# Reordering the opening of a hybrid encoder kernel: x first, small loads on three queues, gate products turned round

## The reference

```
hn = rms_norm(h, norm_mix[0])            # h = x
proj = hn @ w_in                         # 2048 x 12352: q, k, v, z, and 32 + 32 gate columns b, a
qkv = silu(causal_depthwise_conv(qkv, conv_w))       # 4 taps
q = l2_normalize(q); k = l2_normalize(k)
beta = sigmoid(b)
g = -exp(a_log) * softplus(a + dt_bias)
o = gated_delta_rule_chunked(q, k, v, g, beta)       # uses cumulative sums of g
```

## Time and profile before

| | us |
|---|---|
| median of 3 runs | 3359.17 (3358.46 to 3363.18) |
| profiled execution, its time | 3362.38 |
| its span in the trace | 3360.7 |
| PE busy | 3197.1 (95% of the span) |
| DVE busy | 2268.7 (68%) |
| ACT busy | 1694.3 (50%) |
| POOL busy | 807.8 (24%) |

### The profile page before, as it was taken

The page is one execution under the profiler, slowest core; times in us unless marked ns, Lnnn a source line. Parts: engine busy times, 40 slices in busy tenths (PEclk is TensorE's granted clock), DMA queues, the critical chain, the costliest instruction groups (busy, mean ns, idle before and its releaser), DMA issues.

```text
span 3360.7 us, 62145 instructions
## 1 busy us (share of the span) xinstructions
PE 3197.1 (95%) x19134; PEld 2793.7 (83%) x19134; DVE 2268.7 (68%) x4217; ACT 1694.3 (50%) x3583; POOL 807.8 (24%) x1362
## 2 busy tenths in 40 slices
PE   5999999999989999999999988988999999999987
PEld 5898989898878888888888876877888888888875
DVE  4677777777755688667877756865667655775555
ACT  3556565666654555444545545324555444554443
POOL 0000000000010288788888810761000000000000
PEclk7999999999999999999999999988999999999998
DMA  4444444444347777777777856996666676666743
GB/s 124 117 114 130 113 122 115 123 111 131 106 135 192 193 198 207 196 219 194 204 208 192 213 153 166 269 236 174 178 186 184 180 187 177 186 187 179 187 123 112
DMA packets 1061823, 564.78 MB, mean 168 GB/s; under 512 B 59536, under 2 KB 1049744, under 8 KB 1061232
## 3 DMA queue, kind: packets, MB, share of 16 engines
q1 hardware_dynamic: 995808, 500.79, 55.6%
q10 hardware_dynamic: 57568, 37.50, 3.8%
q0 software_dynamic: 8368, 25.51, 2.5%
HBM read 532.49 MB, written 31.23 MB: 168 GB/s over the span
## 4 chain that ended last, share of the span: by engine, by line
PE 76%; DVE 9%; DMA 7%; issue 4%; ACT 3%; SPq 2%; ACTq 0%; DVEq 0%; POOL 0%; POOLq 0%
PE bank L288 42%; PE bank L289 21%; PE bank L665 5%; DVE w_lo L276 4%; DMA raw<-in_ple_w_gate_dram 3%; DMA z_scratch<-z 2%; ACT w_hi L270 1%; DVE normed L1923 1%; DVE tiles L1911 1%; PE bank L663 1%; DVE tiles L303 1%; SPq L491 1%; SPq L505 1%; ACT mid L968 1%; PE bank L726 0%
## 5 line engine op out<-in xcount | busy, mean ns | idle before, releaser
L288 PE MATMUL bank<-act,w_hi 128*128 128x512 f32 x4352 | 1594.6, 408 | 54.0 <-DVE w_lo L276 41.6
L276 DVE TENSOR_TENSOR w_lo<-raw,w_hi 128x512 fp32r<-128x512 f32 x1856 | 1298.6, 748 | 244.0 <-ACT w_hi L270 232.1
L289 PE MATMUL bank<-act,w_lo 128*128 128x256 f32 x4352 | 1223.4, 281 | 0.0
L288 PE MATMUL bank<-mid,w_hi 128*128 128x512 f32 x3072 | 1096.9, 401 | 27.7 <-DVE mid L1925 13.5
L270 ACT ACTIVATE w_hi<-raw 128x512 fp32r<-128x512 f32 x1856 | 1038.9, 619 | 145.4 <-PE bank L289 65.5
L288 PEld LDWEIGHTS bank<-act,w_hi 128*128 128x128 f32 x4352 | 825.1, 190 | 258.8 <-DVE w_lo L276 57.1
L289 PE MATMUL bank<-mid,w_lo 128*128 128x256 f32 x3072 | 866.3, 282 | 0.0
L289 PEld LDWEIGHTS bank<-act,w_lo 128*128 128x128 f32 x4352 | 828.8, 190 | 4.0 <-issue 3.8
L288 PEld LDWEIGHTS bank<-mid,w_hi 128*128 128x128 f32 x3072 | 583.4, 190 | 171.9 <-DVE mid L1925 14.7
L289 PEld LDWEIGHTS bank<-mid,w_lo 128*128 128x128 f32 x3072 | 586.7, 191 | 0.0
L298 ACT ACTIVATE tiles<-bank 128x256 f32<-128x256 f32 x384 | 145.4, 379 | 574.7 <-PE bank L289 572.0
(11 more groups left out here) (311 smaller groups left out, 2995.6 us busy)
## 6 DMA issues: line engine op xcount, KB each, us to landing
raw<-in_mlp_w_up_dram SPq DMA_DIRECT2D x128, 1024.0 KB, 6.4
raw<-in_mlp_w_down_dram SPq DMA_DIRECT2D x128, 1024.0 KB, 6.0
raw<-in_gdn_w_in_dram SPq DMA_DIRECT2D x96, 1024.0 KB, 5.8
raw<-in_gdn_w_out_dram SPq DMA_DIRECT2D x32, 1024.0 KB, 6.2
raw<-in_ple_w_gate_dram SPq DMA_DIRECT2D x32, 1024.0 KB, 6.0
raw<-in_s_w_out_dram SPq DMA_DIRECT2D x28, 1024.0 KB, 6.8
raw<-in_s_w_in_dram ACTq DMA_DIRECT2D x10, 1024.0 KB, 11.8
c_scratch<-c_pow ACTq DMA_DIRECT2D x32, 256.0 KB, 4.4
```

Of the source, the lines that this page charges most:

```text
L276: eng.tensor_tensor(w_lo[par][:, c], raw[slot][:, c], w_hi[par][:, c].bitcast(F32), ALU.subtract).then_inc(S("lo_ready"), 1)
L288: eng.matmul(a[:, :], w_hi[par][:, w], rhs[:, k0 + kt, :], start=(k0 + kt == 0), stop=False)
L289: mm = eng.matmul(a[:, 0:NT], w_lo[par][:, w], rhs[:, k0 + kt, 0:NT], start=False, stop=(k0 + kt == kend - 1))
```

## The change

It rewrites the opening only; from the first round of the main loop on the instructions are the same.

- **Loads.** SP loads x in two halves with the constants between them, then chunks 0 and 1. ACT's queue takes nine small loads: three for S5 (`lam_in`, together with the constants) and six vectors (`params_in`). POOL's queue takes ten: the convolution taps, the gate weights, biases and masks (`side_in`).
- **x.** Scaled x goes to a buffer of its own (`xs`) and is turned first; raw x is turned after chunk 1, with h0 copied by ACT then.
- **Gates.** High and low gate weights lie side by side as one 128-column stationary operand, the 512 columns of `act` stream past: 16 matmuls. ACT copies the result out, and four small matmuls against a doubled identity (`cf[:, 15, :]`) turn it back and add the parts, after the first quarter of chunk 0.
- **S5 parameters.** DVE does a first part before x is scaled, a second beside chunk 0 and the gate values, and the rest after splitting chunk 2.
- **Order.** The sums of g come after chunk 1 and raw x, their transpose after the second quarter of chunk 2. Chunks 1 and 2 are split ahead of the loop over chunks; in it chunk n+3 is split after the convolution of chunk n (on DVE) and ahead of the tanh (on ACT). `gcT` is copied by ACT before it splits chunk 3.

Cut to its core:

```diff
...
+LAM_PARAMS, N_PARAMS, SIDE_PARAMS = 4, 6, 10
...
+        sb("four_pairs", [P, 4, 2 * NT], F32, g4b)
+        ba_out = sb("ba_out", [P, 2 * NT], F32, g4b)
+        xs = sb("xs", [P, 2, D], F32, g4b)
+        h0 = sb("h0", [P, KT, NT], F32, g4b)
...
+        ba_hl = mid[:, 0:4, :].rearrange("p a n -> p (a n)").rearrange("p (k s n) -> p k s n", k=KT, s=2)
...
+            x_rows = t["x"][0].rearrange("(b p) d -> b p d", p=P)
+            sp.dma_start(xn[:, 0, :], x_rows[0]).then_inc(S("x_in"), 16)
+            sp.dma_start(consts[:, :], t["constants"][:, 0:256]).then_inc(S("lam_in"), 16)
+            sp.dma_start(xn[:, 1, :], x_rows[1]).then_inc(S("x_in1"), 16)
             for n, col in enumerate((0, 2048, 4096, 4096 + P)):
                 if n == 2:
                     sp.wait_ge(S("ba_lo"), 1)
...
-            pe.wait_ge(S("params_in"), 16 * N_PARAMS)
-            for i in range(4):
...
+            def turn_x(src, again):
+
...
+                    if g >= 4:
+                        pe.wait_ge(*((S("h0_ready"), g - 3) if again else (S("act_ready0"), 2 * (g - 4) + 2)))
...
+                                              src[:, b, (2 * g + a) * P:(2 * g + a + 1) * P], ident)
                     mm.then_inc(S("x_turned"), 1)
+
+            pe.wait_ge(S("lam_in"), 16 * LAM_PARAMS)
+            pe.transpose(F[:, 0:P], rows[:, 3, :], ident)
+            pe.wait_ge(S("steps_ready"), 1)
+            pe.transpose(F[:, P:P + 64], rows[0:64, 4, :], ident[0:64, 0:64]).then_inc(S("vectors_turned"), 1)
+            pe.wait_ge(S("params_in"), 16 * N_PARAMS)
+            pe.transpose(A[:, 0:P], rows[:, 0, :], ident).then_inc(S("vectors_turned"), 1)
+            pe.wait_ge(S("x_scaled"), 2)
+            turn_x(xs, False)
+            pe.wait_ge(S("side_in"), 16 * SIDE_PARAMS)
+            for i in (1, 2):
+                mm = pe.transpose(A[:, i * P:(i + 1) * P], rows[:, i, :], ident)
+            mm.then_inc(S("vectors_turned"), 1)
 
             pe.wait_ge(S("act_ready0"), KT)
...
-            pe.wait_ge(S("vectors_ready"), 2)
...
-                for kt in range(KT):
-                    x_hi, x_lo = act[:, kt, b * P:(b + 1) * P], act[:, kt, NT + b * P:NT + (b + 1) * P]
-                    pe.matmul(A[:, b * 64:(b + 1) * 64], x_hi, bh[:, kt, :], start=(kt == 0), stop=False)
-                    pe.matmul(A[:, b * 64:(b + 1) * 64], x_lo, bh[:, kt, :], start=False, stop=False)
-                    mm = pe.matmul(A[:, b * 64:(b + 1) * 64], x_hi, bl[:, kt, :], start=False, stop=(kt == KT - 1))
+            pe.wait_ge(S("vectors_ready"), 3)
+            for kt in range(KT):
+                mm = pe.matmul(A[:, :], ba_hl[:, kt, :, :].rearrange("p s n -> p (s n)"), act[:, kt, :], start=(kt == 0),
+                               stop=(kt == KT - 1))
             mm.then_inc(S("ba_done"), 1)
...
+            def ba_turn():
+
+                pe.wait_ge(S("ba_out"), 2)
+                for b in range(2):
+                    for half_ in range(2):
+                        mm = pe.matmul(A[:, b * 64:(b + 1) * 64], ba_out[:, half_ * NT + b * P:half_ * NT + (b + 1) * P],
+                                       cf[:, 15, :], start=(half_ == 0), stop=(half_ == 1))
+                mm.then_inc(S("ba_done"), 1)
...
                     multiply(pe, n, q, n % 2, n % 2, act, tile_free=(n - 1) if (n >= 2 and q == 0) else None)
-                if n == 0:
-
-                    pe.wait_ge(S("setup_vectors"), 7)
+                    if n == 0 and q == 0:
+                        ba_turn()
+                    if n == 2 and q == 1:
+                        pe.wait_ge(S("setup_vectors"), 8)
+                        pe.transpose(F[0:64, 0:P], ga[:, 0, :], ident).then_inc(S("gc_turned"), 1)
+                if n == 1:
+                    turn_x(xn, True)
+                    pe.wait_ge(S("setup_vectors"), 6)
+                    pe.wait_ge(S("h0_ready"), 8)
                     g_all = ga[:, 8, :]
                     pe.matmul(B[:, 0:64], U, g_all, start=True, stop=True)
                     pe.matmul(B[:, 64:128], ones, g_all, start=True, stop=True).then_inc(S("gc_done"), 1)
-                if n == 1:
-                    pe.wait_ge(S("setup_vectors"), 8)
-                    pe.transpose(F[0:64, 0:P], ga[:, 0, :], ident).then_inc(S("gc_turned"), 1)
                 if n == 2:
...
+            params = [(rows[0:64, 3, :], t["s5_lam_re"][0].rearrange("(q g) p -> q (g p)", g=2), "lam_in"),
+                      (rows[64:128, 3, :], t["s5_lam_im"][0].rearrange("(q g) p -> q (g p)", g=2), "lam_in"),
+                      (ls2[0:64, 0:2], t["s5_log_step"][0].rearrange("(q g) -> q g", g=2), "lam_in"),
...
+            for dst, src, name in params:
+                se.dma_start(dst, src, allow_slow_non_contiguous=dst.shape[-1] == 1).then_inc(S(name), 16)
+            se.wait_ge(S("vectors_turned"), 1)
+            link(A_(cf[:, 0:2, :].rearrange("p a b -> p (a b)"), F[:, 0:P]))
+            A_(cf[:, 2, :], F[:, P:P + 64], ACT.Exp).then_inc(S("vectors_ready"), 1)
             for b in range(2):
+                se.wait_ge(S(("x_in", "x_in1")[b]), 16)
...
-            A_(bh, ba_w[:, :]).then_inc(S("ba_hi"), 1)
+            A_(vec[:, :], A[:, 0:P]).then_inc(S("vectors_ready"), 1)
+            for q in range(QUARTERS):
+                split_hi(se, 0, q, 0, 1, reused=False, par=0)
...
+                se.wait_ge(S("x_turned"), kt // 2 + 1)
...
+            se.wait_ge(S("side_in"), 16 * SIDE_PARAMS)
+            A_(ba_hl[:, :, 0, :], ba_w.rearrange("p (k n) -> p k n", k=KT)).then_inc(S("ba_out"), 1)
+            for q in range(QUARTERS):
+                split_hi(se, 1, q, 1, 1, reused=False, par=1)
+            se.wait_ge(S("vectors_turned"), 3)
+            A_(conv_w[:, :, :].rearrange("p a b -> p (a b)"), A[:, P:3 * P]).then_inc(S("vectors_ready"), 1)
+            se.wait_ge(S("ba_done"), 1)
+            A_(ba_out[:, :], A[:, :]).then_inc(S("ba_out"), 1)
...
-            se.wait_ge(S("ba_done"), 1)
+            A_(abias[:, 2, :], abias[:, 0, :], ACT.Exp).then_inc(S("setup_functions"), 1)
+            se.wait_ge(S("ba_done"), 2)
             v = A[:, 0:P].rearrange("p (b k h) -> p b k h", b=2, k=2)
             gv = lambda i: ga[:, i, :].rearrange("p (b h) -> p b h", b=2)
             A_(gv(0), v[:, :, 0, :], ACT.Exp, scale=-1.0).then_inc(S("setup_functions"), 1)
-            A_(abias[:, 2, :], abias[:, 0, :], ACT.Exp).then_inc(S("setup_functions"), 1)
+            se.wait_ge(S("setup_vectors"), 4)
+            A_(ga[:, 5, :], ga[:, 4, :], ACT.Exp, scale=-1.0).then_inc(S("setup_functions"), 1)
             se.wait_ge(S("setup_vectors"), 5)
...
             A_(ga[:, 6, :], ga[:, 5, :], ACT.Ln).then_inc(S("setup_functions"), 1)
+            for q in range(QUARTERS):
+                split_hi(se, 2, q, 2, 1, par=0)
+            se.wait_ge(S("setup_vectors"), 3)
+            A_(cf[:, 11, :], cf[:, 10, :], ACT.Sin)
+            A_(cf[:, 12, :], cf[:, 10, :], ACT.Sin, scale=0.5).then_inc(S("setup_functions"), 1)
+            A_(cf[:, 13, :], cf[:, 13, :], ACT.Sin).then_inc(S("setup_functions"), 1)
+            for g in range(8):
+                se.wait_ge(S("x_turned"), 8 + g + 1)
+                se.wait_ge(S("x_squared"), 2)
+                A_(h0[:, 2 * g:2 * g + 2, :].rearrange("p k n -> p (k n)"), (C, Dk, E, F)[g % 4][:, :]).then_inc(S("h0_ready"), 1)
...
-            for n in range(4):
-                for q in range(QUARTERS):
-                    split_hi(se, n + 1, q, (n + 1) % 3, (n + 1) // 3 + 1, reused=n + 1 >= 2, par=(n + 1) % 2)
...
+            for n in range(3):
+                half_copy(se, n + 1, n, n % 2, first=n < 2)
+                if n == 0:
+                    se.wait_ge(S("gc_turned"), 1)
+                    A_(gcT[0:64, :], F[0:64, 0:P]).then_inc(S("gc_turned_out"), 1)
                 if n < 2:
+                    for q in range(QUARTERS):
+                        split_hi(se, n + 3, q, (n + 3) % 3, 2, par=(n + 3) % 2)
                     gate_tanh(n, n % 2, y[:, n, :], "conv_done", n + 1, n < 2)
                 if n == 1:
                     squares(0, 2)
-                    se.wait_ge(S("gc_turned"), 1)
-                    A_(gcT[0:64, :], F[0:64, 0:P]).then_inc(S("gc_turned_out"), 1)
                 if n == 2:
+                    inverse_lengths(0, False)
                     decays(0)
...
+            side += [(ba_w.rearrange("p (k n) -> p k n", k=KT), w_in_d[:, :, 12288:12352]),
...
+            for dst, src in side:
+                gp.dma_start(dst, src, allow_slow_non_contiguous=dst.shape[-1] == 1).then_inc(S("side_in"), 16)
...
+            ve.wait_ge(S("lam_in"), 16 * LAM_PARAMS)
...
-            ve.wait_ge(S("x_squared"), 3)
-            link(ve.reciprocal(stat[:, 4:6], stat[:, 2:4]))
-            ve.wait_ge(S("x_turned"), 8)
-            for b in range(2):
-                TS(xn[:, b, :], xn[:, b, :], stat[:, 4 + b:5 + b], None, ALU.mult).then_inc(S("x_scaled"), 1)
...
-            ve.wait_ge(S("vectors_ready"), 2)
```

(57 more changed lines are left out.)

121 lines of the change are left out of this document (24 added, 97 removed).

## The result

The changed kernel takes 3341.33 us (median of 6 runs, 3328.85 to 3348.04) beside 3358.82 for the kernel before (6 runs, 3346.95 to 3365.65). The ratio is 0.9947, 95% interval 0.9922 to 0.9973: 17.8 us faster, 9 to 26 (the ratio applied to 3358.82). The forecast was 3336 in a range of 3331 to 3343.

What follows compares the result with a forecast made beforehand. The bound was when the main loop's first transpose starts, PE being busy from 108.5 us on. Earlier gate start 17.5 plus shorter gates 14.2 less 8.1 behind them gave 23.6 us: 3336, range 3331 to 3343.

Steps and rivals of the forecast that it cites:

- First term: Opening, before the root: the three S5 loads on ACT's queue land at 7.5 us, bounds 6.1 to 8.4.
- Rival (a): First stretch: S5 loads, parameters or chunk 0 held up by x, plus Exp's table; 3 to 5 us later, 3339 to 3341; 0.15.
- the queues: Small loads off SP's queue: exactly issue time is saved, the 11.6 us between 0.9 and 12.50.
- Second term: From the gates' end to the main loop's first transpose: 48.8 us instead of 40.7, 8.1 lost.
- The new order: Behind the gates: the rearranged work makes that stretch 48.8 us instead of 40.7, a loss of 8.1.
- Both waits: PE idles some 7 us between chunk 1 and chunk 2, and 7 us before the squared lengths, queued ahead of chunk 3.
- The tables: ACT's table loads take 1.28 us each, with no added drain of 1.38 us.
- the 3343 of that rule: Five table loads on the new chain with a 1.38 us drain each: up to 6.9 us longer, 3343; left out.
- The step that failed: Main loop's first transpose: whatever it moves forward is gained in the whole run; 23.6 us.
- the last of the signs of being wrong: Whole run: the forecast is wrong if the main loop's first transpose (L663) moved and the span did not.

Runs made afterwards that it cites:

- experiment 3: The changed kernel with all 19 small loads back on SP's queue, behind x and ahead of the chunks: 3354.82 us (one run).
- experiment 4: The changed kernel with one move each: squared lengths behind chunk 3 (3346.28 us), last 18 S5 instructions later (3335.50), raw x turned in two halves (3321.98).
- s5_late: The changed kernel with DVE's last 18 S5 instructions moved behind the first convolution: 3335.50 us (one run).
- experiment 6: The changed kernel with every first load held back until DVE has done 35 additions: 3365.76 us, beside 3337.66 unchanged and 3356.44 for the kernel before.
- held kernel: The changed kernel with every engine's first load waiting for 35 additions on DVE: 3365.76 us (12 runs), ratio 1.0024 to the kernel before.
- Experiment 7: The changed kernel with GpSimd's S5 load burst waiting until SP has issued its fifth gate-weight load: 3340.46 us (6 runs), ratio 0.9937 to the kernel before.
- lengths_later: The changed kernel with the squared lengths' two products moved behind chunk 3 on PE: 3346.28 us (8 runs), ratio 0.9946 to the kernel before.
- experiment 5: The changed kernel's opening rearranged to fill idle time: 3322.13 us, ratio 0.9883 to before; then with inverse lengths ahead of the decays: 3322.25 us, ratio 0.9894.
- raw early: The changed kernel with raw x turned in two halves, one ahead of the gates, and copied in ACT's idle time: 3321.98 us (one run).
- lengths first: The changed kernel with its opening rearranged to fill idle time and ACT's inverse lengths ahead of the decays: 3322.25 us (5 runs), ratio 0.9894 to before.

## Why the prediction was right, and where it was not

**The sum.** Opening 23.6 predicted, 23.8 in the first pair of traces, 23.3 in the mean. Step by step, and with G the end of the gates:

| step | predicted | measured |
|---|---|---|
| S5 loads there | 7.5 (6.1 to 8.4) | 10.5 |
| load of Exp's table | 0 or 1.28, a quarter taken | 0 |
| root ready | 15.2 | 17.3 |
| chunk 0 lands | 12 to 17, needed 15.8 | 18.3, needed 17.4 |
| activations done | 27.0 | 28.7 |
| gates start | 29.8 | 30.8 |
| gates take | 6.3 | 6.4 to PE's next row |
| G | 36.1 | 37.3 |
| chunk 0 and 1 to | G + 12.0 | G + 12.2 |
| S5 list ends | G + 18.0 | G + 17.6 |
| copies of h0 | G + 12.7 to 17.0 | G + 12.8 to 16.9 |
| PE idle ahead of chunk 2 | some 7 | 4.6 (1.15 and 3.47) |
| chunk 2 starts | G + 21.2 | G + 21.1 |
| squared lengths | G + 36.9, PE idle 7 | G + 36.4, PE idle 6.81 |
| main loop | G + 48.8 | G + 47.4 |
| `gcr` awaited | no | no |

**First term mis-sized.** "I take 7.5, nearer to tcol": the S5 loads landed 3.0 us later, outside the bounds of 6.1 to 8.4, and experiment 3 shows that the queue doesn't matter. The bounds came from two loads, alone and beside x; neither was a small load issued between larger ones. Rival (a) was so the true course of the first stretch, with two thirds of its cause: the loads at 10.5, chunk 0 at 18.3. It cost 1.2 us at G and not 3 to 5. At the root 2.1 of the 3.0 are left: Exp's table wasn't needed (0.3 of it stood in the sum), and the sum itself is 0.3 too long (8.5 + 0.5 + 3.78 + 0.2 + 1.28 + 0.3 is 14.6 and not 14.9). When ACT starts on the gate weights, at 27.2 where the forecast has 26, 1.2 are left. That the measured 3341 is the price of rival (a) is chance: the opening didn't lose those 5 us.

**Mis-sized beside it, the queues.** "What is saved is exactly issue time, the 11.6 us between 0.9 and 12.50": it was saved, and 3.8 of it arrived (experiment 3), since a chunk issued at 2.31, beside x, took 16.0 us to land, and one issued at 14.02 took 8.1. The early root comes from the order, S5 loads and x first, and not from the queues.

**Second term mis-sized.** The stretch behind G came out 1.4 us shorter than 48.8: squared lengths 0.5 early, and 11.1 us from there to the milestone in place of 11.9 (chunk 3 took 7.4, not 7.8). The turning of raw x takes PE 3.66 us there, so that less of the stretch is idle than forecast, at no cost. (By its own terms the working gives 27.4 us from chunk 2 to the milestone, not 27.6, and 6.8 for cold gates, not 6.9; nothing hangs on either.) Two errors of opposite sign make the agreement of 84.9 and 84.71 better than the working was.

**Right with its mechanism.** The new order costs 8.1 us behind the gates by the forecast (6.7 measured). Both waits stand where they were put, and experiment 4 shows each to be what it was called: the one ahead of chunk 2 two chains that end together, the one ahead of the squared lengths a wait of chunk 3 for a product that it doesn't need. The prediction named DVE's list as the later of the two chains by 1 us (G + 18.0 against 17.0). In after DVE's list ends at 54.92 and then waits 0.77 us for ACT, whose table and exponential follow its copies (to 55.66), and s5_late shows that ACT's chain alone holds the rest.

**Right, by the runs.** The tables: the next row starts 1.29 us behind each load's start (15.69 and 16.98), and the load starts within 0.02 us of the end of the row ahead (50.10 + 4.03 and 54.14), so there is no room for a drain on either side. With a drain of 1.38 us for each, as the Trainium skill has it ("ScalarE: Activation LUTs", What ACT_TABLE_LOAD costs), ACT's chain to G + 16.9 would not fit. That the measured 3341 lies nearer to the 3343 of that rule is chance, for the milestone is the one without drains. The queues: the two kernels of experiment 3 differ by 3.3 us, by the landing of chunk 0, and the S5 loads land no later when all stand on one; the sentence of the Trainium skill ("Trainium Kernel Development and Optimization", Key Constraints) that several queues save issue time only agrees.

**The step that failed.** "Whatever it moves forward is gained, whatever else the change does." The 3336 stands on it, and the measured 3341 is the difference, though the first comparison alone (9 to 26 us) has room for 23.6. In three comparisons 18 us (14 to 22) arrive of 23.3, and in the first pair of traces the span shrank by 14.4 where the milestone moved by 23.8, which comes near the last of the signs of being wrong that were named ahead. An earlier start isn't punished (experiment 6), but the instruction streams meet again at one place, 1.9 ms later, where two engines' loads are issued within tenths of a microsecond to 2 us of each other, and in all three traces of after, and in the held kernel, they meet in the worse order. Experiment 7 shows that the order makes the long wait. What that is worth is known less well: 6 us between the two groups' means, 3.9 in the one trace in which it was turned round, and in the run times nothing that can be told from their scatter. So the 5 us that are missing have a candidate of the right size and no proof. In its favour: lengths_later, with GpSimd first, is 18 us under before where its milestone gives 25, while the two rearranged kernels of experiment 5, with SP first, are 39 and 36 us under before where theirs give 34.4 and 38.7 (each time known to 6 to 8 us). The kernel made to test it, with 21 us (13 to 29) of 23.2, fits either account. Why SP's third gate weight, and with it the fifth, comes late in after, when s5_late, which differs from it by the place of 18 small instructions, has it early, is open. So is the rest of the scatter of some 10 us: the S5 part behind that stage (238 to 248 us in all the traces) varies as much.

**Not seen.** The gates' clock (3.87 to 6.77 us for the same 16 products) and the time left in the new opening. The listed waits were on record as costs and not as room: filling them gives 11.2 and 15.5 us more than the change, by the milestones of experiment 5, of which 1.1 and 2.7 are the gates' clock and not the order.

## What to carry to other kernels

Behind a shortened stage, write down for each engine when it becomes free, and look for two chains that end together: moving one of them alone gained 0 and 1.2 us here, filling the idle time of both, with the other moves of experiment 5, 11. A gain in the opening is counted to its milestone; whether it reaches the end depends on places where two queues' loads are issued almost together, so look for these in the trace. A semaphore fixes their order, and here took the long wait away; that it shortens the whole was not measured. Judge a few microseconds by milestones over several traces, not by one pair of whole times.

## What the runs showed of the hardware

- **A small load isn't quick.** 0.5 KB issued at 2.20 and 8 KB issued at 5.8, with x, the constants and chunk 0 on the wires, took 8.3 and 9.7 us to land. Before, the 0.5 KB issued at 9.81, when x had landed, took 2.7. With all small loads on SP's queue `log_step` was there at 10.35, with three queues at 10.40 to 10.99 (nine traces).
- **The order of two issues decides by microseconds.** 1 MB issued 0.4 us ahead of a burst of 2.3 MB lands in 9.8 us, 0.4 us behind its first load in 14.3 us, and 1.05 us ahead of it in 6.2 us; the ranges over fourteen traces stand in experiment 7.
- **The same 16 products of 512 columns took 3.89 us at a granted clock of 1.00 and 6.60 at 0.55.** PE had stood idle 4.37 us ahead of the slow ones and 1.57 and 1.71 us, behind 3 us of transposes, ahead of the fast ones (raw early, lengths first). A third kernel with the same work in front and 1.66 us of idle time took 5.48 at 0.69, and the held kernel with 4.62 us of idle time 5.50 at 0.69, so the idle time alone doesn't fix it.
